# Later gather: selection columns written after all passes are planned, and zero fills moved from GpSimd to VectorE, in a decoder step with top-2-of-8 experts

## The chip, the cores and the metric

One core of a Trainium2 chip runs the whole program. The metric is device time in microseconds (us) of one execution, the median of several. The engines are TensorE (PE), VectorE (DVE), ScalarE (ACT), GpSimd (POOL) and the SyncE queue (SP) that issues most of the loads.

## What is computed

One inference step of two layers for 272 prompt rows (16 meta tokens and 256 tokens) and 8 sample rows, 280 rows of width 1024 in all. Layer 0 is a state-space and sparse-attention mixer with a dense SwiGLU. Layer 1 is a pooling mixer and then the part that matters here, a top-2-of-8 expert SwiGLU:

```
logits = (t @ router_w)                       # t: the normed rows, (280, 1024)
top_v, top_i = lax.top_k(logits, 2)
gates = jax.nn.softmax(top_v, axis=-1)
dense_gate = sum(one_hot(top_i, 8) * gates[..., None], axis=1)
for e in range(8):                            # expert width 3584
    out = out + dense_gate[:, e:e + 1] * (silu(t @ w_gate[e]) * (t @ w_up[e])) @ w_down[e]
```

## The kernel before

Rows are kept in three chunks (TC = 3) of 128, 128 and 24. The expert part works in passes. A pass takes up to 128 rows that chose one expert, so there are at least 8 passes, and up to 4 more where an expert has over 128 rows; the number is computed on the chip (`n_pass`). In a pass TensorE gathers the rows by a matmul with a 0/1 selection matrix `pick`, runs them through 84 blocks of weights, each split into a high and a low fp32r part (ScalarE copies the high part, L1502; VectorE subtracts it to get the low part, L2046; three matmuls each use them, L1153, L1157, L1158), and scatters the result back in the next pass through `pickTr`. The gather for pass i+1 is done inside pass i. The gather for pass 0 is done ahead of the loop, and it is this stretch that the change touches.

Each engine has its own instruction stream, written out by hand, with semaphores between them. `link(...)` on VectorE makes each small instruction wait for the one before. `filled(eng, x)` waits until TensorE has filled the PSUM bank of x, and `emptied(eng, x)` until that bank has been read. The streams before the loop, in their own order:

- VectorE: top-2 of the router logits (L1963 to L1974), then the low parts of the normed rows `hn4` (L1982); wait for `rank`, a running count of the rows of each expert (a matmul of TensorE, L1098); the place of each row within its expert, `slot_v` (L1986 to L1988); the selection columns `pick` for pass 0 from `slot_v` (L1990, three instructions), which signals `pick_ready`; the softmax gates (L1993 to L1998), which need the exponential of ScalarE (L1475, signal `router_exp`); the plan of the passes, in `pslot`, `pgate` and `exp_i` (L2002 to L2024), which signals `passes_ready`; the low parts of the gathered rows (L2029), which need ScalarE's high parts; a register load of the number of passes (L2039); the loop.
- TensorE: router logits (L1079); transposes of the normed rows into `h2n` (L1089); `rank` (L1098); transposes of the residual rows into `xn` (L1089 again); wait for `pick_ready`; gather half 0 and half 1, 20 matmuls each (L1108); wait for `late_zeros`; two matmuls on zeros that fill the `y` banks (L1133); wait for `passes_ready` and load the number of passes (L1134, L1135); the loop.
- ScalarE: high parts of `hn4` (L1473); the exponential (L1475); six copies of `xn` into the accumulator (L1480, by the helper at L1251); wait for gather half 0, high part; wait for gather half 1, high part (L1484); wait for `passes_ready`, load the number of passes (L1488, L1489); the loop, which begins with five high parts of weight blocks (L1502).
- GpSimd: waits until the last two `xn` banks are read, sets `pickTr` (128x384) and `ybr` (128x2048) to zero (L726, L727) and signals `late_zeros`.
- SP: the first 7 loads of expert weights (1 MB each) are issued before this stretch, so the loop's first blocks lie ready; the rest is issued as blocks are used.

Of the kernel before, what the change touches and what calls it, by code (L numbers as in the profile page):

```python
# [16 lines left out]
F32 = mybir.dt.float32  # L17
# [3 lines left out]
ALU = mybir.AluOpType  # L21
# [9 lines left out]
TC = 3  # L31
# [11 lines left out]
NE = 8  # L43
# [198 lines left out]
LOW_ROWS = 32  # L242
PASSES_EXTRA = 4
PASSES = NE + PASSES_EXTRA
# [36 lines left out]
def hybrid_step(nc, a, o):  # L281

    with ExitStack() as ctx:
        sems = {}

        def sem(name):
            if name not in sems:
                sems[name] = ctx.enter_context(nc.semaphore(name))
            return sems[name]
# [17 lines left out]
        pickTr = sb("pickTr", TC * P, F32R)  # L307
# [4 lines left out]
        ybr = sb("ybr", 2 * D, F32R)  # L312
# [8 lines left out]
        def const(name):  # L321
            at, n = CONST_AT[name]
            return consts[:, at:at + n]
# [18 lines left out]
        ident, ones, iota = const("ident"), const("ones"), const("iota")  # L342
# [107 lines left out]
        pick = pickr[:, :].rearrange("p (t s) -> p t s", t=TC)  # L450
# [13 lines left out]
        pslot = tk((PASSES + 1) * TC).rearrange("p (i t) -> p i t", i=PASSES + 1)  # L464
# [17 lines left out]
        def filled(eng, name):  # L482

            eng.wait_ge(bank_full[bank_of(name)], bank_uses(name))

        def emptied(eng, name):

            eng.wait_ge(bank_free[bank_of(name)], bank_uses(name))
# [29 lines left out]
        def ps(name):  # L518
            return bank[bank_of(name)]
# [156 lines left out]
        @block.gpsimd  # L676
        def _(pool):
            done = [0]

            def link(ins):  # L680

                done[0] += 1
                ins.then_inc(sem("pool_step"), 1)
                pool.wait_ge(sem("pool_step"), done[0])

            TT = nc.gpsimd.tensor_tensor
            nc.gpsimd.memset(eps, EPS)
            nc.gpsimd.memset(qibd, 0.0).then_inc(sem("zeroed"), 1)
            pool.wait_ge(sem("consts_in"), 16)
            nc.gpsimd.tensor_copy(hexp[0:H, :].rearrange("p (h m) -> p h m", h=H), ident[0:H, 0:H].unsqueeze(2).to_broadcast([H, H, HD]))  # L690
            nc.gpsimd.tensor_copy(hrep[0:H, :].rearrange("p (b h) -> p b h", b=NB),
                                  ident[0:H, 0:H].unsqueeze(1).to_broadcast([H, NB, H])).then_inc(sem("spread"), 1)

            pool.dma_start(o["pool_s"][:, 0:14, :], a["state_pool"][:, 1:15, :]).then_inc(sem("pool_old_out"), 16)

            for j in range(NJ):
                emptied(pool, ("bui", j))
                emptied(pool, ("bur", j))
                gr, gi = g4[:, j % 2, 0, :], g4[:, j % 2, 1, :]
                TT(pt[0], er3[:, j, :], gr, ALU.mult)  # L700
                TT(pt[1], ei3[:, j, :], gi, ALU.mult)
                TT(pt[2], er3[:, j, :], gi, ALU.mult)
                link(TT(pt[3], ei3[:, j, :], gr, ALU.mult))
                TT(er3[:, j, :], pt[0], pt[1], ALU.subtract)
                TT(ei3[:, j, :], pt[2], pt[3], ALU.add).then_inc(sem("states"), 1)
                pool.wait_ge(sem("states"), j + 1)

            emptied(pool, "kidT")
            for t in range(TC):
                pool.dma_start(o["kidx"][t * P:t * P + TCN[t], :], z3["kid"][0:TCN[t], t, :]).then_inc(sem("ki_out"), 16)  # L710
            for t in range(TC):
                for n, name in (("v", ("v", t)), ("k", ("kt", t))):
                    emptied(pool, name)
                    pool.dma_start(o[n][t * P:t * P + TCN[t], :], z3[n][0:TCN[t], t, :]).then_inc(sem("kv_out"), 16)
            filled(pool, ("y", 3))
            nc.gpsimd.memset(psbd, 0.0).then_inc(sem("probs_zeroed"), 1)
            pool.wait_ge(sem("sample_state"), 1)
            pool.dma_start(o["hs"], hs.rearrange("p j r b -> p (j r b)")).then_inc(sem("state_out"), 16)
            pool.wait_ge(sem("last_state"), 1)
            pool.dma_start(o["hl"], hlast).then_inc(sem("state_out"), 16)  # L720
            pool.wait_ge(sem("mixer_over"), 1)
            emptied(pool, "svT")
            pool.dma_start(hist.rearrange("p c b r -> p (c b r)"), a["hist"]).then_inc(sem("hist_in"), 16)
            for i in range(2):
                emptied(pool, ("xn", 2, i))
            nc.gpsimd.memset(pickTr[:, :].bitcast(F32), 0.0)  # L726
            nc.gpsimd.memset(ybr[:, :].bitcast(F32), 0.0).then_inc(sem("late_zeros"), 1)  # L727

        @block.tensor
        def _(pe):  # L730
# [819 lines left out]
        def _(dve):  # L1550
# [3 lines left out]
            def link(ins):  # L1554

                done[0] += 1
                ins.then_inc(sem("dve_step"), 1)
                dve.wait_ge(sem("dve_step"), done[0])
# [418 lines left out]
            for t in range(TC):  # L1977
                for i in range(2):
# [2 lines left out]
                    low_rows = hn4[0:n, 1, t, cols] if t < 2 else hn4[LOW_ROWS:LOW_ROWS + n, 0, t, cols]  # L1981
                    TT(low_rows, ps(("h2n", t, i))[0:n, :], hn4[0:n, 0, t, cols].bitcast(F32),  # L1982
                       ALU.subtract).then_inc(free(("h2n", t, i)), 1)
            filled(dve, "rank")
            rp = ps("rank")[:, 0:4 * NE].rearrange("p (t e) -> p t e", t=4)
            link(TT(slot_v, sel, rp[:, 0:TC, :], ALU.mult))  # L1986
            link(TS(slot_v, slot_v, -1.0, None, ALU.add))
            link(nc.vector.tensor_copy(slot_v[LOW_ROWS:LOW_ROWS + 24, 2, :], slot_v[0:24, 2, :]))  # L1988
            for t in range(TC):
                last = TS(pick[:, t, :], iota, slot_v[:, t, 0:1], None, ALU.is_equal)  # L1990
            last.then_inc(sem("pick_ready"), 1)
            dve.wait_ge(sem("router_exp"), 1)
            link(TS(g12[:, 2, :], g12[:, 1, :], 1.0, None, ALU.add))  # L1993
            link(nc.vector.reciprocal(g12[:, 2, :], g12[:, 2, :]))
# [1 line left out]
            link(TT(oh1, oh1, g12[:, 2, :].unsqueeze(2).to_broadcast([P, TC, NE]), ALU.mult))  # L1996
            link(TT(oh2, oh2, g12[:, 3, :].unsqueeze(2).to_broadcast([P, TC, NE]), ALU.mult))
            link(TT(gate, oh1, oh2, ALU.add))  # L1998

            ov2 = over.rearrange("p (b e) -> p b e", b=2)  # L2000
            for b in range(2):
# [11 lines left out]
            for dst, src, first in ((pslot[:, 0:PASSES, :], cand, slot_v), (pgate[:, 1:PASSES + 1, :], gcand, gate)):  # L2013
# [3 lines left out]
                link(nc.vector.tensor_reduce(dst[:, NE:PASSES, :].rearrange("p i t -> p t i"), prod, AX.X, ALU.add))  # L2017
                link(nc.vector.tensor_copy(dst[:, 0:NE, :].rearrange("p e t -> p t e"), first))
            link(TT(prod[:, 0, :, :], const("ecol").unsqueeze(1).to_broadcast([P, 4, 16]), oh, ALU.mult))
            link(nc.vector.tensor_copy(pexp[:, 0:NE], iota[:, 0:NE]))  # L2020
            link(nc.vector.tensor_reduce(pexp[:, NE:PASSES], prod[:, 0, :, :], AX.X, ALU.add))
            link(nc.vector.tensor_copy(exp_i[:, 0:PASSES], pexp))
            link(TS(over[:, 0:1], ranko[:, 15:16], float(NE), None, ALU.add))
            nc.vector.tensor_copy(exp_i[:, PASSES:PASSES + 1], over[:, 0:1]).then_inc(sem("passes_ready"), 1)  # L2024
            dve.wait_ge(sem("passes_ready"), 1)
            for half in range(2):
                cs = slice(4 * half, 4 * half + 4)
                dve.wait_ge(sem("high_copied"), half + 1)
                TT(xg4[:, 1, cs, :], bank[PASS_BANK[("gather", half)]][:, :].rearrange("p (c s) -> p c s", c=4),  # L2029
                   xg4[:, 0, cs, :].bitcast(F32), ALU.subtract).then_inc(bank_free[PASS_BANK[("gather", half)]], 1)  # L2030
# [162 lines left out]
```

## Time and profile before

| | us |
|---|---|
| median of 3 runs | 1674.99 |
| lowest, highest | 1674.94, 1676.63 |
| profiled execution, its time | 1674.94 |
| profiled execution, its span | 1673.1 |
| TensorE busy | 1566.4 (94%) |
| VectorE busy | 1272.2 (76%) |
| ScalarE busy | 963.8 (58%) |
| GpSimd busy | 89.3 (5%) |

The profile is of one execution. Its times count from the start of the span; 1.8 us of the execution's own time lie outside the span. "L1990" is a line of the kernel before. PEclk is the granted clock of TensorE, where 1.00 is 2.4 GHz and 0.50 is 1.2 GHz.

### The profile page before, as it was taken

Reading aid. Unit: us, or ns where it says so; the run is one execution under the profiler, and the core shown is the slowest. Engines: PE = TensorE matmul, PEld = TensorE weight load, DVE = VectorE, ACT = ScalarE, POOL = GpSimd, SP = SyncE. Lnnn points to the kernel's source line nnn. Section 1 sums busy time; section 2 is a strip of 40 time slices with the busy share of each in tenths; the row PEclk is TensorE's granted clock in tenths of the full one; section 3 lists DMA queues with packets and bytes.
Section 4 is the critical chain, followed back from the end, with each engine's and each line's share of the span. In section 5 each row is a group of like instructions: output and inputs, shape, how many; then the busy total and the mean of one; then the engine's idle time right before and its main releaser. Section 6 shows DMA issues by size and latency. Waiting matters only on the chain.

```text
span 1673.1 us, 23394 instructions
## 1 busy us (share of the span) xinstructions
PE 1566.4 (94%) x7789; PEld 1263.8 (76%) x7789; DVE 1272.2 (76%) x1702; ACT 963.8 (58%) x1222; POOL 89.3 (5%) x120
## 2 busy tenths in 40 slices
PE   5997858889999878999999999999999999999998
PEld 4653436479999767888888888888888888888887
DVE  8888561135554469988988988988998998988986
ACT  2110314124443227777777777777777777777774
POOL 0386100000000000000000000000000000000000
PEclk9998778999999979999999999999999999999999
DMA  5421012524545516998998998998998998998992
GB/s 219 151 76 51 30 54 64 150 101 152 193 128 173 180 59 241 361 363 311 358 373 301 355 369 307 355 374 309 346 366 320 351 366 319 348 363 323 350 357 92
DMA packets 212886, 420.79 MB, mean 252 GB/s; under 512 B 10233, under 2 KB 56469, under 8 KB 212572
## 3 DMA queue, kind: packets, MB, share of 16 engines
q1 hardware_dynamic: 211542, 414.37, 68.9%
q10 hardware_dynamic: 622, 3.45, 0.5%
q0 software_dynamic: 672, 2.32, 0.4%
q8 instruction: 30, 0.49, 0.1%
q14 instruction: 20, 0.16, 0.0%
HBM read 417.50 MB, written 3.07 MB: 251 GB/s over the span
## 4 chain that ended last, share of the span: by engine, by line
PE 83%; DVE 4%; issue 2%; ACT 1%; DMA 1%; SPq 1%; ACTq 0%; DVEq 0%
PE bank L1153 19%; PE bank L1158 19%; PE bank L1157 19%; PE bank L1034 3%; PE bank L1031 3%; PE bank L1035 3%; PE bank L1108 2%; PE bank L1014 2%; PE bank L1178 1%; PE bank L1116 1%; PE bank L1046 1%; PE bank L1050 1%; PE bank L1049 1%; PE bank L748 1%; PE bank L922 1%
## 5 line engine op out<-in xcount | busy, mean ns | idle before, releaser
L2046 DVE TENSOR_TENSOR split<-raw_w,split 128x1024 fp32r<-128x1024 f32 x672 | 783.3, 1220 | 50.3 <-ACT split L1502 48.2
L1502 ACT ACTIVATE split<-raw_w 128x1024 fp32r<-128x1024 f32 x672 | 684.2, 1059 | 109.1 <-PE bank L1153 108.1
L1153 PE MATMUL bank<-split,xgr 128*128 128x512 f32 x896 | 359.2, 401 | 6.0 <-DVE split L2046 6.0
L1158 PE MATMUL bank<-split,xgr 128*128 128x512 f32 x896 | 354.3, 395 | 0.0
L1157 PE MATMUL bank<-split,xgr 128*128 128x512 f32 x896 | 354.2, 395 | 0.0
L1153 PEld LDWEIGHTS bank<-split,xgr 128*128 128x128 f32 x896 | 169.3, 189 | 43.8 <-DVE split L2046 6.4
L1158 PEld LDWEIGHTS bank<-split,xgr 128*128 128x128 f32 x896 | 169.0, 189 | 39.9
L1157 PEld LDWEIGHTS bank<-split,xgr 128*128 128x128 f32 x896 | 169.4, 189 | 37.5
L1153 PE MATMUL bank<-split,hbr 128*128 128x512 f32 x448 | 177.9, 397 | 0.0
L1158 PE MATMUL bank<-split,hbr 128*128 128x512 f32 x448 | 176.9, 395 | 0.0
L1157 PE MATMUL bank<-split,hbr 128*128 128x512 f32 x448 | 176.9, 395 | 0.0
L1031 PE MATMUL bank<-split 128*128 128x280 f32 x352 | 103.6, 294 | 6.5 <-DVE split L1902 6.5
L1035 PE MATMUL bank<-split 128*128 128x280 f32 x352 | 103.4, 294 | 0.0
L1034 PE MATMUL bank<-split 128*128 128x280 f32 x352 | 103.3, 294 | 0.0
L1428 ACT ACTIVATE split<-ring 128x1024 fp32r<-128x1024 f32 x44 | 46.4, 1059 | 92.3 <-PE bank L1031 70.5
L1158 PEld LDWEIGHTS bank<-split,hbr 128*128 128x128 f32 x448 | 84.3, 188 | 20.0
L1153 PEld LDWEIGHTS bank<-split,hbr 128*128 128x128 f32 x448 | 84.3, 188 | 19.3
L1157 PEld LDWEIGHTS bank<-split,hbr 128*128 128x128 f32 x448 | 84.3, 188 | 19.2
L1892 DVE TENSOR_TENSOR split<-ring,split 128x1024 fp32r<-128x1024 f32 x44 | 53.8, 1226 | 51.1 <-ACT split L1428 51.1
L2052 DVE TENSOR_TENSOR hbr<-bank,hbr 128x512 fp32r<-128x512 f32 x56 | 38.6, 690 | 49.3 <-ACT hbr L1507 49.3
L1532 ACT ACTIVATE late<-bank 128x512 f32<-128x512 f32 x56 | 33.5, 598 | 71.4 <-PE bank L1158 71.4
L1031 PEld LDWEIGHTS bank<-split 128*128 128x128 f32 x352 | 67.2, 191 | 6.9 <-issue 6.9
(377 smaller groups left out, 1904.2 us busy)
## 6 DMA issues: line engine op xcount, KB each, us to landing
raw_w<-in_moe_gate SPq DMA_DIRECT2D x112, 1024.0 KB, 5.4
raw_w<-in_moe_up SPq DMA_DIRECT2D x112, 1024.0 KB, 6.1
raw_w<-in_moe_down SPq DMA_DIRECT2D x112, 1024.0 KB, 5.1
ring<-in_w_gate SPq DMA_DIRECT2D x11, 1024.0 KB, 5.0
ring<-in_w_up SPq DMA_DIRECT2D x11, 1024.0 KB, 7.3
ring<-in_w_down SPq DMA_DIRECT2D x8, 1408.0 KB, 6.2
ring<-in_w_in SPq DMA_DIRECT2D x5, 2048.0 KB, 9.6
ring<-in_w_out SPq DMA_DIRECT2D x2, 2048.0 KB, 7.8
```

The source lines that it names most:

```text
L1031: first = mm(out[:, 0:T], w[0][:, c, :], xs[:, 0, c, :], start=(c == 0), stop=False)
L1034: mm(out[:, 0:T], w[0][:, c, :], xs[:, 1, c, :], start=False, stop=False)
L1035: last = mm(out[:, 0:T], w[1][:, c, :], xs[:, 0, c, :], start=False, stop=(c == C - 1))
L1153: first = mm(out, hi, place[:, s, 0, cols], start=start, stop=False)
L1157: mm(out, lo, place[:, s, 0, cols], start=False, stop=False)
L1158: last = mm(out, hi, place[:, s, 1, cols], start=False, stop=stop)
L1428: A(place[:, n % FF_PLACES, 0, :].rearrange("p (c m) -> p c m", c=C), unit(name, 256)[:, k * C:(k + 1) * C, (f % 2) * P:(f % 2) * P + P], ...
L1502: A(place[:, s, 0, :], raw_w[:, at:at + BLOCK], ACT.Copy).then_inc(sem("high_ready"), 1)
L1532: A(th[:, j % 2, :], bank[b][:, :], ACT.Silu).then_inc(bank_free[b], 1)
L1892: TT(low_, unit(f"ffn{f // 2}", 256)[:, k * C:(k + 1) * C, (f % 2) * P:(f % 2) * P + P], high.bitcast(F32), ALU.subtract).then_inc(sem("ff ...
L2046: TT(place[:, s, 1, :], raw_w[:, at:at + BLOCK], place[:, s, 0, :].bitcast(F32), ALU.subtract).then_inc(sem("low_ready"), 1)
L2052: TT(dst, src, high.bitcast(F32), ALU.subtract).then_inc(bank_free[PASS_BANK[name]], 1)
```

## The change

On VectorE the gate arithmetic now comes before the wait for `rank`. `slot_v` is computed after it. The plan of the passes follows as before, with one copy of 24 rows made on `pslot` in place of the one made on `slot_v`. Only after `passes_ready` are the selection columns of pass 0 written, now read from `pslot`, and `pick_ready` signalled. Then VectorE, in place of GpSimd, waits for the two `xn` banks and sets `pickTr` and `ybr` to zero. The low parts of the gathered rows follow. The streams of TensorE, ScalarE and SP are as before.

```
@@ gpsimd
             pool.dma_start(hist.rearrange("p c b r -> p (c b r)"), a["hist"]).then_inc(sem("hist_in"), 16)
-            for i in range(2):
-                emptied(pool, ("xn", 2, i))
-            nc.gpsimd.memset(pickTr[:, :].bitcast(F32), 0.0)
-            nc.gpsimd.memset(ybr[:, :].bitcast(F32), 0.0).then_inc(sem("late_zeros"), 1)
@@ vector
-            filled(dve, "rank")
-            rp = ps("rank")[:, 0:4 * NE].rearrange("p (t e) -> p t e", t=4)
-            link(TT(slot_v, sel, rp[:, 0:TC, :], ALU.mult))
-            link(TS(slot_v, slot_v, -1.0, None, ALU.add))
-            link(nc.vector.tensor_copy(slot_v[LOW_ROWS:LOW_ROWS + 24, 2, :], slot_v[0:24, 2, :]))
-            for t in range(TC):
-                last = TS(pick[:, t, :], iota, slot_v[:, t, 0:1], None, ALU.is_equal)
-            last.then_inc(sem("pick_ready"), 1)
             dve.wait_ge(sem("router_exp"), 1)
             link(TS(g12[:, 2, :], g12[:, 1, :], 1.0, None, ALU.add))
...
             link(TT(gate, oh1, oh2, ALU.add))
+
+            filled(dve, "rank")
+            rp = ps("rank")[:, 0:4 * NE].rearrange("p (t e) -> p t e", t=4)
+            link(TT(slot_v, sel, rp[:, 0:TC, :], ALU.mult))
+            link(TS(slot_v, slot_v, -1.0, None, ALU.add))
...
             link(TT(prod[:, 0, :, :], const("ecol").unsqueeze(1).to_broadcast([P, 4, 16]), oh, ALU.mult))
+            link(nc.vector.tensor_copy(pslot[LOW_ROWS:LOW_ROWS + 24, 0:PASSES, 2], pslot[0:24, 0:PASSES, 2]))
             link(nc.vector.tensor_copy(pexp[:, 0:NE], iota[:, 0:NE]))
...
             nc.vector.tensor_copy(exp_i[:, PASSES:PASSES + 1], over[:, 0:1]).then_inc(sem("passes_ready"), 1)
             dve.wait_ge(sem("passes_ready"), 1)
+            for t in range(TC):
+                last = TS(pick[:, t, :], iota, pslot[:, 0, t:t + 1], None, ALU.is_equal)
+            last.then_inc(sem("pick_ready"), 1)
+            for i in range(2):
+                emptied(dve, ("xn", 2, i))
+            nc.vector.memset(pickTr[:, :].bitcast(F32), 0.0)
+            nc.vector.memset(ybr[:, :].bitcast(F32), 0.0).then_inc(sem("late_zeros"), 1)
             for half in range(2):
                 cs = slice(4 * half, 4 * half + 4)
                 dve.wait_ge(sem("high_copied"), half + 1)
```

## Rows read from the trace of the kernel before

**Rows 1.** The page's busy time of each engine, with share and instructions

```profile
PE 1566.4 (94%) x7789; PEld 1263.8 (76%) x7789; DVE 1272.2 (76%) x1702; ACT 963.8 (58%) x1222; POOL 89.3 (5%) x120
```

**Rows 2.** Busy time by stretch, one pass; columns as in the first line

```profile
core 0: us, PE busy (x) PEld busy (x) DVE busy (x) ACT busy (x) POOL busy (x), PEclk, DMA share, GB/s
752.00:880.00 128.00, 128.00 (x589) 104.65 (x588) 113.20 (x114) 97.57 (x106) 0.00 (x0) 1.00 0.94 345
```

**Rows 3.** Chain that ended last, 625 to 644 us: start, length, engine, tile, line

```profile
625.11 0.19 DVE late L1986
...
625.54 0.17 DVE late L1988
...
625.73 0.68 DVE pickr L1990 x3
626.41 0.09 DVE late L1993
...
633.82 0.17 DVE small_i L2024
...
634.00 0.47 ACTq L1489
...
636.29 1.07 ACT split L1502
...
637.38 1.24 DVE split L2046
...
638.66 0.79 PE bank L1153
639.45 0.43 PE bank L1157
...
643.73 0.23 PE bank L1153
```

**Rows 4.** Timeline of ScalarE, 622 to 635 us; [idle before, released by]

```profile
622.72 1.07 ACT L1473 ACTIVATE hnr<-bank 24x512 fp32r<-24x512 f32 x2 [0.26 <-PE bank L1089]
623.80 1.28 ACT L1475 ACT_TABLE_LOAD   x1
625.10 0.20 ACT L1475 ACTIVATE late<-late 128x3 f32<-128x3 f32 x1
...
632.20 0.60 ACT L1484 ACTIVATE xgr<-bank 128x512 fp32r<-128x512 f32 x1 [1.63 <-PE bank L1108]
635.00 1.28 ACT L1502 ACT_TABLE_LOAD   x1 [2.20 <-issue]
```

**Rows 5.** Timeline of TensorE, 618 to 633 us

```profile
618.15 5.01 PE L1089 MATMUL bank<-consts,hT 128*128 128x128 f32 x24
...
624.93 2.82 PE L1089 MATMUL bank<-consts,xT 128*128 128x128 f32 x24
627.50 4.66 PE L1108 MATMUL bank<-pickr,hnr 128*128 128x128 f32 x40
632.00 0.68 PE L1133 MATMUL bank<-ybr 128*128 128x512 f32 x2
```

**Rows 6.** Busy time by stretch, columns as in rows 2, where PEclk changes

```profile
604.00:605.00 1.00, 0.47 (x2) 0.03 (x1) 0.00 (x0) 0.49 (x1) 0.00 (x0) 1.00 0.92 332
...
609.00:610.00 1.00, 0.00 (x0) 0.00 (x0) 1.00 (x4) 0.00 (x0) 0.00 (x0) 0.50 0.00 0
...
622.00:623.00 1.00, 1.00 (x8) 0.72 (x6) 0.91 (x2) 0.74 (x2) 0.00 (x0) 0.68 0.00 0
...
636.00:636.50 0.50, 0.00 (x0) 0.00 (x0) 0.00 (x0) 0.49 (x2) 0.00 (x0) 0.80 0.00 0
...
643.00:643.50 0.50, 0.50 (x3) 0.36 (x2) 0.50 (x2) 0.50 (x2) 0.00 (x0) 0.87 1.08 422
```

**Rows 7.** Timeline of VectorE, a large zero fill and the gathered low parts

```profile
610.92 1.76 DVE L1954 MEMSET hnr<- 128x2048 f32 x1 [0.49 <-DVE hT L1565]
...
634.00 1.29 DVE L2029 TENSOR_TENSOR xgr<-bank,xgr 128x512 fp32r<-128x512 f32 x2
```

**Rows 8.** VectorE's sequencer at L2039: count, ns, first and last start

```profile
L2039 DVEq TENSOR_LOAD <-small_i x1: 552/552/552, 634.0 to 634.0; - x1
```

## The prediction, made before the changed kernel ran

> **What bounds the kernel now.** I read the page first: TensorE is busy 94% of the span, VectorE 76% [rows 1]. An average hides stages, so I then took the busy time by stretch over each pass of the expert loop. Seven stretches of a pass each, from 752 to 1648 us, read alike; one of them stands in the rows: TensorE is busy 128.00 of 128 us at full clock [rows 2]. The loop is bound by TensorE and has no gap that could absorb a late start. DMA is at 0.94 of its share there, close to a bound, but it never leaves TensorE idle. So whatever moves the first expert matmul, at 638.66 us, moves the end by the same amount.
>
> Then I read the chain of waits that ends in that first matmul [rows 3]. It runs on VectorE alone from 625.11 (first use of `rank`) to the end of L2024 at 633.97, which signals `passes_ready`. From there: ScalarE loads the number of passes (634.00), loads an activation table from 635.00 to 636.28 [rows 4], makes the first high part (636.29, 1.07), VectorE makes its low part (637.38, 1.24), and TensorE starts at 638.66. From signal to matmul that is 638.66 - 633.97 = 4.69 us.
>
> The gather of pass 0 is not on that chain. `pick` is ready at 626.41 [rows 3], the gather runs from 627.50 to 632.16 [rows 5], and ScalarE's second copy ends at 632.80 [rows 4], 1.2 us before `passes_ready`. The planning of the passes hides the gather. That cover is what the change takes away.
>
> **The change part by part.**
>
> *The planning chain, up to `passes_ready`.* Removed between `rank` and `passes_ready`: the copy of 24 rows and the three selection instructions, from 625.54 to the start of the gate arithmetic. L1993 began inside the last selection: the chain shows 0.09 us of it after 626.41, and an instruction of its size takes about 0.17 (L1988), so it began near 626.33. That is 0.79 us [rows 3]. Added: a copy of 24 rows on `pslot`, which I price like the old one with its hand-over, 0.2 [rows 3]; and a wait, since the gates now come first and need the exponential, which ends at 625.10 + 0.20 = 625.30 [rows 4] where `rank` let the chain start at 625.11 [rows 3], so 0.2. Behind that waiting instruction on VectorE stands all the planning, so all of it shifts. The order of gates and `slot_v` among themselves costs nothing, as every instruction is linked to the one before either way. Net: -0.79 + 0.2 + 0.2 = -0.4, and `passes_ready` comes at 633.6.
>
> *The selection columns.* Now behind `passes_ready`, three instructions, 0.68 us as before [rows 3]. They read another tile of the same kind. `pick_ready`: 633.6 + 0.02 + 0.68 = 634.3. TensorE wakes about 0.04 later (the step from L2046 to L1153 in the chain [rows 3]), so the gather starts at 634.35 in place of 627.50.
>
> *The gather.* 40 matmuls. At full clock they took 4.66 us, 0.1165 each [rows 5]. But TensorE has now been idle since the `xn` transposes ended at 627.75 [rows 5], 6.6 us. The granted clock went to 0.50 by 609.0 after a last matmul at 604.47, so within 4.5 us, and at 636.30 after TensorE ended at 632.68, so after 3.6 us [rows 5, 6]. 6.6 us is more than both, so the gather starts at 1.2 GHz. The clock came back at 622.64 (a mean of 0.68 over that us is 0.64 us at 0.50 and 0.36 at 1.00; the other times are read in the same way) and at 643.13 [rows 6], about 4.5 us after dense work began at 618.15 [rows 5] and at 638.66 [rows 3]. No gather at low clock stands in the trace. The nearest rows are the 24 transposes of the same width, 128 columns: at full clock 2.82 us, 0.1175 each, which is what a gather matmul costs there; and 5.01 us for the 24 that began at 618.15 [rows 5]. Of these, those after 622.64, some 0.5 us and 4 matmuls, ran at full clock, so 20 or 21 took 4.5 us, 0.218 each. I take 0.218 for the gather. In 4.5 us that makes 20.6 matmuls; the other 19.4 at 0.1165 take 2.3. Sum 6.8 us, and the gather ends at 634.35 + 6.8 = 641.15. The bounds: 4.7 if the clock is high throughout, 8.7 if it is low throughout.
>
> *From the gather to the loop.* ScalarE's stream has the two gather copies ahead of its wait for `passes_ready`, so it is stuck there until the second half is in its bank. Behind it are the register load, the table load and every high part of the loop; behind those are VectorE's low parts and TensorE. The second copy starts at 641.2. Does the register load wait for this 0.60 us copy? VectorE's sequencer did its own load at 634.0 [rows 8] while L2029 was computing from 634.00 to 635.29 [rows 7], so a sequencer runs ahead of its engine, and I take it that the copy hides the register load's start. From 641.2 the same 4.69 us as before follow (register load, table, high part, low part): first expert matmul at 645.9. If the sequencer does not run ahead, add 0.6.
>
> For that table load the Trainium skill ("ScalarE: Activation LUTs", What ACT_TABLE_LOAD costs) states a drain of about 1.38 us besides the load's 1.28. The trace does not agree: the load at 623.80 begins as the copies of `hn4` end at 623.79, and the exponential follows it at 625.10 [rows 4]. By the page's figure the load would come an estimated 0.9 us later here, because ScalarE is now busy just before it.
>
> *Zero fills.* Off GpSimd's and onto VectorE: 128x2048 took VectorE 1.76 us [rows 7], so with 128x384 in proportion 2.1 us, from 634.3 to 636.5. The banks they wait for are read long before. Behind them on VectorE stand the low parts of the gathered rows, but these need ScalarE's copies at 641 to 642; hidden by the gather. Without that cover they would cost the 2.1. The low parts then end near 642.5, and TensorE wants them at 645.9; hidden by ScalarE's table load. The two matmuls on zeros (L1133) follow the gather within 0.7 us [rows 5]; hidden too, as is TensorE's own register load.
>
> *The loop's start.* Before, about ten matmuls ran at 0.43 in place of 0.23 until the clock rose [rows 3], 2 us lost. After the change TensorE idles from about 641.7 to 645.9, 4.2 us, which is longer than one of the two idle times after which the clock fell (3.6) and shorter than the other's bound (4.5) [rows 5, 6]. I take the fall as likelier, with the same 2 us lost: no difference.
>
> **Sum.** 645.9 - 638.66 = +7.2 us. Made up from the pieces: gather end moves from 632.16 to 641.15 (+9.0), and of this the 1.8 us by which the old gather ended ahead of `passes_ready` are eaten up first. On the profiled execution's 1674.94 that is 1682.1; the median shown is 1674.99, so it is the same for it.
>
> **Rivals.**
>
> *The clock stays up (not as far as I say).* The 4.2 us of idling before the loop do not bring the clock down, so the ten slow matmuls at the start run at 0.23. For it: the gather now sits right before the loop, and one fall came only by 4.5 us. Against it: the other came after 3.6. Price -2.0: 1680.1. A part of it, an earlier rise in the loop or in the gather, lies between.
>
> *A longer way from gather to loop.* The register load waits for the copy (+0.6), or the gather stays at low clock throughout (+1.9). For it: there is no row of a gather at low clock. Against it: the sequencer row, and both rises came 4.5 us after dense work began. 1682.7 to 1684.0.
>
> *The late gather is hidden anyway (not slower).* If something else held the loop back until after the gather, only the shorter planning chain would count: -0.4, 1674.6. This decides if the gather's second half is in its bank by 633.6, or if the loop could give the time back. For it: DMA is at 0.94 in the loop, so a ring of weights that has had more time to fill is the only thing that gains. Against it: the ring is already full at the start, TensorE has no idle time in any pass [rows 2], and the gather would have to end before `pick` exists.
>
> **How the numbers follow.** About 0.2% (3.3 us) is what a measurement of this kernel can tell from no change. Chances: my sum, 1681.2 to 1682.6, 0.6; clock up, near 1680, 0.2; longer way 0.12; hidden 0.05, within 0.2%; something that I don't see 0.03. The range that leaves out less than 2 in 10 is 1679.7 to 1684.1: its low end is the clock's rival less a little for an early rise in the gather, its high end the gather at low clock throughout. Slower by over 0.2% means above 1678.3, which takes in the first three cases: 0.93. Same 0.05, faster 0.02.
>
> **What would show it.** In the changed profile: `passes_ready` 0.3 to 0.5 us earlier; L1108's first 40 matmuls starting near 634.4 with a PEclk of 0.50 for the first 4 to 5 us; ScalarE's second gather copy near 641.2; its table load near 642 and not before; the first L1153 near 645.9; passes of unchanged length after that; the zero fills on VectorE ended before the gather is. The prediction would be wrong if the gather started at full clock, if ScalarE loaded the number of passes ahead of its gather copies, or if a pass of the loop became shorter or longer.

## The result and the profile after

The changed kernel is slower: 1689.7 us median of four timed runs (1686.3 to 1692.9) against 1675.8 for the kernel before (one run more than in the table above), a ratio of 1.0081 with a 95% interval of 1.0054 to 1.0108. Timed again in six runs beside the kernel before in 23, it took 1688.3 against 1677.4, ratio 1.0063 (1.0041 to 1.0085). The forecast was 1682.1 with a range of 1679.7 to 1684.1. The direction was right, the size was not. The profiled execution took 1684.85 us, 9.91 more than that of before.

Line numbers differ a little from those of the kernel before: the gather is now L1104, the first expert matmul L1149, ScalarE's gather copies L1480, the loop's high parts L1498.

The page's busy times of the changed kernel, to be set beside [rows 1]: TensorE runs the same 7789 matmuls, so the added time is waiting and low clock.

```profile
PE 1571.4 (93%) x7789; PEld 1268.0 (75%) x7789; DVE 1274.4 (76%) x1704; ACT 963.7 (57%) x1222; POOL 87.2 (5%) x118
```

The chain that ended last, changed kernel, 625 to 645 us (start, length, engine, tile, line):

```profile
625.39 0.21 ACT late L1471
...
625.62 0.18 DVE late L1981
...
626.89 0.19 DVE late L1990
...
633.74 0.17 DVE small_i L2018
...
633.93 0.04 DVE pickr L2021
...
634.62 0.27 issue
634.90 8.78 PE bank L1104 x40
643.68 0.02 issue
643.70 0.48 ACT xgr L1480
```

In [rows 3] this chain was VectorE's planning alone and the gather was not on it. Now it starts with the exponential (L1471), runs through the gates (L1981) and the planning to L2018, and then through the gather, which alone is 8.78 us.

TensorE over the same stretch, changed kernel:

```profile
610.99 7.73 PE L1075 MATMUL bank<-params,hT 128*128 128x8 f32 x48 [6.01 <-DVE hT L1561]
618.66 4.75 PE L1085 MATMUL bank<-consts,hT 128*128 128x128 f32 x24
623.25 2.07 PE L1094 MATMUL bank<-late,consts 128*128 128x8 f32 x18
625.18 2.82 PE L1085 MATMUL bank<-consts,xT 128*128 128x128 f32 x24
634.90 8.77 PE L1104 MATMUL bank<-pickr,hnr 128*128 128x128 f32 x40 [6.90 <-DVE pickr L2021]
643.46 1.16 PE L1129 MATMUL bank<-ybr 128*128 128x512 f32 x2
648.37 0.80 PE L1149 MATMUL bank<-split,xgr 128*128 128x512 f32 x1 [3.75 <-DVE split L2047]
```

Against [rows 5], the 40 matmuls of the gather take 8.77 us in place of 4.66, after 6.90 us in which TensorE waited for the selection columns. The first expert matmul is at 648.37 in place of 638.66.

Busy time by stretch, changed kernel (columns as in [rows 2]): where the clock fell, the gather, where the clock rose, and one pass of the loop.

```profile
632.00:633.00 1.00, 0.00 (x0) 0.00 (x0) 0.86 (x5) 0.00 (x0) 0.00 (x0) 0.93 0.00 0
...
634.90:643.67 8.77, 8.77 (x41) 8.77 (x42) 2.58 (x3) 0.60 (x1) 0.00 (x0) 0.50 0.00 0
...
653.00:654.00 1.00, 1.00 (x6) 0.77 (x5) 1.00 (x3) 1.00 (x2) 0.00 (x0) 0.83 1.05 410
...
763.00:891.00 128.00, 128.00 (x590) 104.65 (x589) 113.20 (x114) 97.48 (x105) 0.00 (x0) 1.00 0.94 344
```

The granted clock is 0.50 over the whole gather, and over everything from 632.86 (a mean of 0.93 over that us) to 653.34. In [rows 6] the fall at 636.30 was followed by a rise at 643.13. The passes of the loop are as in [rows 2].

ScalarE and VectorE after the gather, changed kernel:

```profile
643.70 0.60 ACT L1480 ACTIVATE xgr<-bank 128x512 fp32r<-128x512 f32 x1 [3.67 <-PE bank L1104]
644.71 1.28 ACT L1498 ACT_TABLE_LOAD   x1 [0.41 <-issue]
646.00 4.84 ACT L1498 ACTIVATE split<-raw_w 128x1024 fp32r<-128x1024 f32 x5
```

```profile
634.64 0.38 DVE L2025 MEMSET pickTr<- 128x384 f32 x1
635.39 1.76 DVE L2026 MEMSET ybr<- 128x2048 f32 x1 [0.38 <-issue]
640.06 0.69 DVE L2030 TENSOR_TENSOR xgr<-bank,xgr 128x512 fp32r<-128x512 f32 x1 [2.90 <-ACT xgr L1480]
644.33 0.69 DVE L2030 TENSOR_TENSOR xgr<-bank,xgr 128x512 fp32r<-128x512 f32 x1 [3.57 <-ACT xgr L1480]
```

The table load begins 1.01 us after the second gather copy began and 0.41 after it ended; from the copy's start to the first expert matmul it is 648.37 - 643.70 = 4.67 us. The zero fills are over at 637.15, long before the low parts can start.

**How profiles are compared here.** Executions differ before this stretch is reached: the router's first matmul (the one after the 6.01 us of idling) came between 610.1 and 618.2 us of the span in the profiles below, also in kernels whose code up to there is that of before. So two distances are used: from the router's first matmul to the first expert matmul, and from it to the end of the span.

| kernel | router's first matmul | to first expert matmul | to end of span |
|---|---|---|---|
| before | 610.48 | 28.18 | 1062.6 |
| changed | 610.99 | 37.38 | 1072.0 |
| changed, profiled again | 614.09 | 37.65 | 1072.5 |

By this the change costs 9.4 us, or 9.9 by its second profile. The two profiles of one kernel differ by 0.3 and 0.5 us, so a single difference of that size between two kernels says little. Of the 9.91 between the two profiled executions, 0.51 arose before the router.

### The profile page after: what moved, and what is told of

It reads as the page before. It is cut to its first block, busy times and chain, and to the rows that moved or that the text cites. A ratio compares the mean times of both kernels' runs of the same rounds, so it can differ in the third digit from the quotient of the medians.

```text
span 1683.0 us, 23394 instructions
## 1 busy us (share of the span) xinstructions
PE 1571.4 (93%) x7789; PEld 1268.0 (75%) x7789; DVE 1274.4 (76%) x1704; ACT 963.7 (57%) x1222; POOL 87.2 (5%) x118
## 4 chain that ended last, share of the span: by engine, by line
PE 83%; DVE 3%; issue 2%; ACT 1%; DMA 1%; SPq 0%; DVEq 0%; ACTq 0%
PE bank L1149 19%; PE bank L1154 19%; PE bank L1153 19%; PE bank L1027 3%; PE bank L1030 3%; PE bank L1031 3%; PE bank L1104 3%; PE bank L1010 2%; PE bank L1174 1%; PE bank L1112 1%; PE bank L1042 1%; PE bank L1046 1%; PE bank L1045 1%; PE bank L744 1%; DVE hT L1561 1%
## 5 line engine op out<-in xcount | busy, mean ns | idle before, releaser
L1498 ACT ACTIVATE split<-raw_w 128x1024 fp32r<-128x1024 f32 x672 | 684.4, 1060 | 109.3 <-PE bank L1149 108.1
L1149 PE MATMUL bank<-split,xgr 128*128 128x512 f32 x896 | 359.2, 401 | 3.7 <-DVE split L2047 3.7
L1149 PEld LDWEIGHTS bank<-split,xgr 128*128 128x128 f32 x896 | 169.3, 189 | 41.9 <-DVE split L2047 4.5
L1149 PE MATMUL bank<-split,hbr 128*128 128x512 f32 x448 | 177.9, 397 | 0.0
L1149 PEld LDWEIGHTS bank<-split,hbr 128*128 128x128 f32 x448 | 84.3, 188 | 19.3
```

The source lines that it names most:

```text
L1149: first = mm(out, hi, place[:, s, 0, cols], start=start, stop=False)
L1498: A(place[:, s, 0, :], raw_w[:, at:at + BLOCK], ACT.Copy).then_inc(sem("high_ready"), 1)
```

## The experiments

Eleven runs follow. Where nothing else is said, the diff is against the changed kernel.

### The changed kernel again

No edit.

> The changed kernel once more, unaltered. The profiled execution of it took 1684.85 us with the clock low in one stretch from 632.9 to 653.3 us of the span, and four timed ones 1686.3, 1687.1, 1692.3 and 1692.9. Theory A (the extra time is the late gather and its clock alone): every execution has the same low stretch of about 20 us, and the times gather within 2 us of 1685. Theory B (the low stretch differs from execution to execution, by whether the clock has come back when the expert loop is under way): the times spread over 5 us and more, and a slower one shows a mean granted clock some 0.002 to 0.004 lower, that is 7 to 14 us more at 1.2 GHz.

Measured: 1688.3 us median, 1684.5 to 1692.6. TensorE in its profile:

```profile
614.09 7.74 PE L1075 MATMUL bank<-params,hT 128*128 128x8 f32 x48 [6.02 <-DVE hT L1561]
...
638.27 8.76 PE L1104 MATMUL bank<-pickr,hnr 128*128 128x128 f32 x40 [6.83 <-DVE pickr L2021]
...
651.74 0.80 PE L1149 MATMUL bank<-split,xgr 128*128 128x512 f32 x1 [3.75 <-DVE split L2047]
```

The gather repeats to 0.01 us, with the clock low throughout, and the low stretch was again 20.5 us (636.7 to 657.1). The first expert matmul is 37.65 us after the router's first. The times spread over 8 us all the same, but so do those of the kernel before timed beside them, 1674.1 to 1682.8. This profiled execution took 1688.44; 3.1 of the 3.6 us above the first one had arisen before the router. Neither theory held as I put it. As theory B has it, the times spread over more than 5 us and the slower executions show the lower mean clock (0.952 at 1692.6 us, 0.957 at 1684.5). But the low stretch around the gather is equally long in both profiles, and most of the difference between them lies ahead of it.

### Only the late selection, fills back on GpSimd

```
@@ gpsimd
+            for i in range(2):
+                emptied(pool, ("xn", 2, i))
+            nc.gpsimd.memset(pickTr[:, :].bitcast(F32), 0.0)
+            nc.gpsimd.memset(ybr[:, :].bitcast(F32), 0.0).then_inc(sem("late_zeros"), 1)
@@ vector
-            for i in range(2):
-                emptied(dve, ("xn", 2, i))
-            nc.vector.memset(pickTr[:, :].bitcast(F32), 0.0)
-            nc.vector.memset(ybr[:, :].bitcast(F32), 0.0).then_inc(sem("late_zeros"), 1)
```

> The changed kernel with its two zero fills back on GpSimd, where they were before; the selection columns of pass 0 stay behind the planning. Theory A (the late gather is the cost): nothing of the loss comes back, first expert matmul at 648.3 us within 0.5, time as the changed kernel's within 1 us. Rival (the fills on VectorE, 2.1 us, ahead of the low parts of the gathered rows are a good part of the cost): 2 us or more faster than the changed kernel.

Measured: 1685.5 us median of six, ratio to before 1.0048 (1.0032 to 1.0064). The median is 2.7 us under that of the changed kernel run again (1688.3), which the expectation had named as the rival's sign. But those six times lie from 1684.5 to 1692.6, and the distances, 37.29 and 1072.0, are those of the changed kernel within 0.1 of its first profile and 0.5 of its second. By the distances the late selection alone carries the whole loss; the position named in the expectation, 648.3, was 647.4, since the router stood 0.9 us earlier.

### Only the fills on VectorE (against the kernel before)

```
@@ gpsimd
-            for i in range(2):
-                emptied(pool, ("xn", 2, i))
-            nc.gpsimd.memset(pickTr[:, :].bitcast(F32), 0.0)
-            nc.gpsimd.memset(ybr[:, :].bitcast(F32), 0.0).then_inc(sem("late_zeros"), 1)
@@ vector
             dve.wait_ge(sem("passes_ready"), 1)
+            for i in range(2):
+                emptied(dve, ("xn", 2, i))
+            nc.vector.memset(pickTr[:, :].bitcast(F32), 0.0)
+            nc.vector.memset(ybr[:, :].bitcast(F32), 0.0).then_inc(sem("late_zeros"), 1)
```

> The kernel before with only the two zero fills moved to VectorE, behind the signal that the passes are planned; the selection columns are written early as before. Theory A: gather at 627.5 to 632.2 us as before, first expert matmul at 638.7 within 0.4 (the low parts of the gathered rows end near 637.5 in place of 635.3, about when the first high part of the loop is ready), time within 0.5 us of the kernel before. Rival (fills on the path): first expert matmul 2 us later, 1677.

Measured: ratio 0.9999 (0.9984 to 1.0013). Distances 28.54 and 1062.9: +0.36 at the first expert matmul, within the 0.4 expected. Its profiled execution took 1682.91 us, and the profile shows that 7.7 us of this lay ahead of the router (618.16 against 610.48).

TensorE's clock in this profile bears on what follows. The same gather ran here at full clock, with 4.53 us of idling behind it in place of the two matmuls on zeros:

```profile
632.66 2.82 PE L1085 MATMUL bank<-consts,xT 128*128 128x128 f32 x24
635.24 4.66 PE L1104 MATMUL bank<-pickr,hnr 128*128 128x128 f32 x40
644.43 1.22 PE L1129 MATMUL bank<-ybr 128*128 128x512 f32 x2 [4.53 <-DVE ybr L2025]
```

The granted clock fell at 640.7 (a mean of 0.85 over the us from 640), only 0.8 us after the gather had ended and 5.2 us after the last transpose. In the five profiles in which TensorE idled after the same transposes (the changed kernel twice, the late selection alone, dense columns, transposes) it fell 4.8 to 5.2 us after the last of them. So in this one profile the clock fell as early as if the gather had not run.

### The changed kernel with a warm gather

```
+            b = PASS_BANK[("gather", 0)]
+            pe.wait_ge(bank_free[b], BEFORE_FILL[b])
+            for _ in range(30):
+                mm(bank[b][:, :], hn4[:, 0, 0, 0:P], hn4[:, 0, 0, 0:512], start=True, stop=True)
             pe.wait_ge(sem("pick_ready"), 1)
```

> The changed kernel with 30 matmuls of 512 columns put into TensorE's idle time between the transposes of the residual rows and the wait for the selection columns; their result is overwritten. At 0.23 us each they take 7 us. If the low clock is what made the gather 8.6 us long, it now takes 4.7 us from near 634.9, the first expert matmul comes 4 us earlier than in the changed kernel, near 644.4, and its time falls by 4 us or more, and if the runs of 1692 us come from the gather as well, the spread goes too. Rival (the gather is long because of its operands or of memory traffic, not of the clock): the gather still takes 8.6 us at a granted clock of 1.00.

Measured: ratio to before 1.0032 (1.0018 to 1.0046), 1682.7 us median. TensorE, and its clock during the gather:

```profile
612.86 7.73 PE L1075 MATMUL bank<-params,hT 128*128 128x8 f32 x48 [6.01 <-DVE hT L1565]
...
629.62 7.07 PE L1123 MATMUL bank<-hnr 128*128 128x512 f32 x30
636.55 4.68 PE L1104 MATMUL bank<-pickr,hnr 128*128 128x128 f32 x40
...
645.93 0.80 PE L1153 MATMUL bank<-split,xgr 128*128 128x512 f32 x1 [4.18 <-DVE split L2051]
```

```profile
636.55:641.23 4.68, 4.68 (x42) 4.68 (x42) 2.81 (x3) 0.60 (x1) 0.00 (x0) 1.00 0.01 4
```

The same gather in the same place takes 4.68 us at full clock, so the low clock is what made them 8.77. Distances 33.07 and 1068.0: 4.3 and 4.0 us come back, where the expectation said 4. The spread did not go (1679.3 to 1688.1), which fits the reading that it has another source.

### Only the gates moved ahead (against the kernel before)

```
+            dve.wait_ge(sem("router_exp"), 1)
+            link(TS(g12[:, 2, :], g12[:, 1, :], 1.0, None, ALU.add))
...
+            link(TT(gate, oh1, oh2, ALU.add))
             filled(dve, "rank")
...
             last.then_inc(sem("pick_ready"), 1)
-            dve.wait_ge(sem("router_exp"), 1)
-            link(TS(g12[:, 2, :], g12[:, 1, :], 1.0, None, ALU.add))
...
-            link(TT(gate, oh1, oh2, ALU.add))
```

> The kernel before with one part of the change alone: the gate arithmetic stands ahead of the wait for the running count, and the selection columns are still written early, right after the places of the rows. Theory A (the order of the planning costs nothing, the late gather everything): the gather starts by 628.5 us (counted with the router's first matmul at 610.5), is over before the planning is, and the time is that of the kernel before within 0.3 us (+0.2 for the wait on the exponential). Rival (the reordering itself delays the planning by 1 us or more): first expert matmul 1 us or more later.

Measured: ratio 0.9996 (0.998 to 1.0012). The gather starts 17.77 us after the router's first matmul, which is 628.25 counted from 610.48; distances 28.50 and 1062.9. By the distances the reordering costs 0.3 us, no more than two profiles of one kernel differ by; the timing, with an interval of 0.16% either way, can't tell it from nothing.

### Dense columns in the late gather

```
-                gather_half(half, bank[b])
+                gather_half(half, bank[b], hn4[:, 0, 0, 0:P])
```

`gather_half` takes this third argument as the moving operand in place of `pick[:, t, :]`.

> The changed kernel with the moving operand of the first gather replaced: the same 40 matmuls of 128 columns read rows of data where the 0/1 selection columns stood, so the first pass gathers sums of no meaning. In two profiled executions of the changed kernel the gather began at 1.2 GHz and ended at 1.2 GHz after 8.6 us, though the clock had come back within 4.5 us of the start of the transposes. Theory C (what the selection columns hold, mostly zeros, is why the clock does not come back): here it comes back within the gather, and the gather takes 6 to 7.5 us. Theory D (it is the form and spacing of these matmuls): 8.6 us at 1.2 GHz again.

Measured: ratio 1.0049 (1.0027 to 1.0072); distances 37.60 and 1072.5. The gather and its clock:

```profile
640.43 8.77 PE L1104 MATMUL bank<-hnr 128*128 128x128 f32 x40 [6.83 <-DVE pickr L2022]
```

```profile
640.43:649.19 8.76, 8.76 (x41) 8.76 (x42) 2.61 (x3) 0.60 (x1) 0.00 (x0) 0.50 0.00 0
```

Theory C falls: what the columns hold made no difference.

### Transposes in place of the late gather

```
-                gather_half(half, bank[b])
+                for k in range(20):
+                    last = nc.tensor.transpose(bank[b][:, (k // 5) * P:(k // 5 + 1) * P],
+                                               hn4[:, 0, 0, 0:P].bitcast(F32), ident)
+                last.then_inc(bank_full[b], 1)
```

> The changed kernel with the 40 matmuls of its first gather replaced by 40 transposes of one 128x128 block of the normed rows, so the first pass gathers no rows. My sum took its rate and its clock from transposes of that width; neither selection columns nor dense columns brought the clock back in a gather. Theory D (the kind of matmul decides): the transposes start at 1.2 GHz after the same idle time, the clock comes back 3.5 to 6 us after their start, and they end within 6 to 7.5 us. Rival (after this idle time nothing brings it back in 8 us): 1.2 GHz to the end, 8.5 us.

One execution, 1687.8 us. The 40 transposes, and two stretches in them:

```profile
640.38 6.91 PE L1125 MATMUL bank<-consts,hnr 128*128 128x128 f32 x40 [6.88 <-DVE pickr L2024]
```

```profile
644.00:645.00 1.00, 1.00 (x7) 1.00 (x6) 0.00 (x0) 0.08 (x1) 0.00 (x0) 0.50 0.00 0
645.00:646.00 1.00, 1.00 (x10) 1.00 (x9) 0.45 (x1) 0.52 (x1) 0.00 (x0) 0.89 0.00 0
```

The clock was low from 638.4, came back at 645.2, 4.8 us after the transposes began, and they took 6.9 us. Theory D held. 6.9 us is what my sum gave for the gather, 6.8. First expert matmul 35.51 us after the router's first, 7.3 more than before; the sum had 7.2. Here the clock, up since 645.2, fell again at 652.0, 4.3 us after the last of the two matmuls on zeros. These transposes differ from the gather in more than one way: they are fp32 where the gather is fp32r, they are issued as transposes, and they use one block throughout where the gather takes a new one each time. The last is hardly it, since the 24 transposes behind the router take a new block each and brought the clock back in every profile. Between the other two nothing decides.

### TensorE kept at work before the loop (against the kernel before)

```
                 mm(bank[b][:, :], yb3[:, 0, 0:P], yb3[:, 0, 0:512], start=True, stop=True).then_inc(bank_full[b], 1)
+            b = PASS_BANK[("gate", 0)]
+            pe.wait_ge(bank_free[b], BEFORE_FILL[b])
+            for _ in range(24):
+                mm(bank[b][:, :], hn4[:, 0, 0, 0:P], hn4[:, 0, 0, 0:512], start=True, stop=True)
```

> The kernel before with 24 matmuls of 512 columns, their result overwritten, put between the two on zeros and the loop, about 5.6 us of work in TensorE's idle time from 632.7 to 638.7. If the low clock at the loop's start (4.5 us in the profile of before) costs what the rows say, it goes, the first expert matmul stays at 638.7 (28.2 us after the router's first), and the end comes 2.0 us earlier, a ratio of 0.9988, which the timing hardly tells from 1; the profile's PEclk of 1.00 from 623 us to the end shows it. Rival (the added matmuls themselves delay the loop): first expert matmul later than 28.5 us after the router's first.

Measured: ratio 0.9984 (0.9968 to 0.9999). No low clock between 626.2 and 1674 us. Distances 28.34 and 1061.6, so 1.0 us comes back at the end where I expected 2.0. The scatter matmuls of the loop (L1116) show where the rest went. Counted from the first expert matmul, the first scatter comes at 5.67 us against 7.71 before, 2.04 earlier, which is the price that I had put on the low clock. The second comes at 12.43 against 14.21, the third at 25.62 against 26.73, 1.11 earlier, and there the difference stays. So 0.9 us is given back within the first 26 us of the loop. The two other kernels with this gap filled have the same third scatter, at 25.62. VectorE is busy 19.88 of the first 20 us there, so its low parts are a likely limit, but that was not tried.

### Both gaps filled in the changed kernel

The 30 matmuls of the warm gather and 17 like those above.

> The changed kernel with TensorE kept at work in both gaps: 30 matmuls of 512 columns before the late gather and 17 between the two on zeros and the loop. If the loss is made up of the gather and its wait in the path (which stays) and of two stretches at low clock (which go), then: first expert matmul 33.1 us after the router's first, as with the first gap filled alone, no low clock after 625 us, and from the router's first matmul to the end of the span some 1.5 to 2.5 us less than with the first gap filled alone (1068.1), so 1065.6 to 1066.6, against 1062.65 before. Rival (the added matmuls delay the loop): first expert matmul later than 33.5.

Measured: ratio 1.0026 (1.0009 to 1.0042). Distances 33.37 and 1066.7, both just above what was expected, and no low clock after 628 us. So without any low clock the late selection still costs 4.1 us against the kernel before, and 5.0 against the kernel before with its own gap filled.

### The opposite of the change (against the kernel before)

```
             last.then_inc(sem("pick_ready"), 1)
-            dve.wait_ge(sem("router_exp"), 1)
...
-            link(TT(gate, oh1, oh2, ALU.add))
             ov2 = over.rearrange("p (b e) -> p b e", b=2)
...
                 link(STT(oh[:, k, :], ranko, float(k + 1), over, ALU.is_equal, ALU.mult))
+            link(TT(prod[:, 0, :, :], const("ecol").unsqueeze(1).to_broadcast([P, 4, 16]), oh, ALU.mult))
...
+            nc.vector.tensor_copy(exp_i[:, PASSES:PASSES + 1], over[:, 0:1]).then_inc(sem("passes_ready"), 1)
+            dve.wait_ge(sem("router_exp"), 1)
...
+            link(TT(gate, oh1, oh2, ALU.add))
             for b in range(2):
                 link(TS(cand[:, :, b, :], slot_v, -128.0 * (b + 1), None, ALU.add))
...
-            link(TT(prod[:, 0, :, :], const("ecol").unsqueeze(1).to_broadcast([P, 4, 16]), oh, ALU.mult))
...
-            nc.vector.tensor_copy(exp_i[:, PASSES:PASSES + 1], over[:, 0:1]).then_inc(sem("passes_ready"), 1)
```

> The opposite of the change: in the kernel before, only what the number of passes and their experts need is computed between the selection columns and the signal that the passes are planned; gates, slots and the rest of the plan follow the signal. Theory A (what sets the loop's start is whichever is later, the gather with its copies or the planning signal, and then 4.7 us): the signal comes near 629.5, the gather copies end at 632.8 as before and the table load follows at once, first high part at 634.1; VectorE is done with its own work near 635.3, so the first expert matmul is near 636.6 in place of 638.7, 2.0 us earlier, and the time falls by 1.5 to 2.5 us. Rival (the 4.7 us are bound to something else, such as the register loads): no gain.

Measured: ratio 0.9988 (0.9971 to 1.0004); distances 26.13 and 1061.2. ScalarE:

```profile
634.09 0.60 ACT L1484 ACTIVATE xgr<-bank 128x512 fp32r<-128x512 f32 x1 [1.38 <-PE bank L1108]
636.32 0.60 ACT L1484 ACTIVATE xgr<-bank 128x512 fp32r<-128x512 f32 x1 [1.64 <-PE bank L1108]
637.32 1.28 ACT L1502 ACT_TABLE_LOAD   x1 [0.40 <-issue]
```

The planning signal now comes at 633.2, ahead of the second gather copy, and the gather has become the later of the two even at full clock. The first expert matmul, at 640.99, is again 4.67 us after the start of that copy. It comes 2.05 us earlier than before, as expected; of that, 1.4 is left at the end. The interval of the timing still takes in 1. The expectation had the signal near 629.5 counted as in the profile of before; it came at 628.8 by that count, also ahead of the gather's end.

### The opposite, with the gap filled

The edit above and 14 matmuls in the gap.

> The kernel before with the number of passes computed first (2.05 us earlier at the first expert matmul) and 14 matmuls of 512 columns in the gap before the loop. It joins two changes that each gave something: router's first matmul to end of span 1061.23 with the first alone, 1061.63 with 24 matmuls in the gap alone. If they add, 1059.5 to 1060.3, and the time 2.5 to 3.5 us under the kernel before, ratio 0.998. Rival (at full clock the first blocks of the loop wait for VectorE's low parts, so the clock gives nothing on top): 1061.2.

Measured: 1675.9 us median against 1677.7, ratio 0.9981 (0.9967 to 0.9995). TensorE:

```profile
613.52 7.74 PE L1079 MATMUL bank<-params,hT 128*128 128x8 f32 x48 [6.01 <-DVE hT L1569]
...
630.58 4.66 PE L1108 MATMUL bank<-pickr,hnr 128*128 128x128 f32 x40
635.08 0.67 PE L1133 MATMUL bank<-ybr 128*128 128x512 f32 x2
635.59 3.38 PE L1137 MATMUL bank<-hnr 128*128 128x512 f32 x14
639.95 0.51 PE L1157 MATMUL bank<-split,xgr 128*128 128x512 f32 x1 [0.98 <-DVE split L2050]
```

Distances 26.43 and 1059.7: 2.9 us under the kernel before and 12.3 under the changed one. The two parts add within 0.5 us. The timed medians show 1.8 us under the kernel before, less than the 2.5 to 3.5 expected, with an interval of 0.8 to 5.5. This version beats both.

## Why the prediction was wrong in size

**The bound and the lost cover: right.** The loop is bound by TensorE and passes a late start on: from first expert matmul to end of span 1034.4 us before, 1034.6 after. The late selection alone gives the whole loss, 37.29 against 37.38, and the fills and the reordering alone give some 0.3 us each, about what two profiles of one kernel differ by.

**The planning chain and the selection: right.** Forecast `passes_ready` 0.4 us earlier: counted from the router it is 0.6 earlier (23.49 to 22.90). The handover to TensorE took 0.3 us, not the 0.04 that I took from a matmul in the loop's chain. The two cancel: gather start 23.9 us after the router's first matmul, forecast and measured.

**The gather: the step that failed.** The sum had the low clock for the first 20.6 of the 40 matmuls: "In 4.5 us that makes 20.6 matmuls; the other 19.4 at 0.1165 take 2.3. Sum 6.8 us". The rate was right, 0.214 each at low clock (634.90 to 643.46) against the 0.218 that I took. The return of the clock was not. I took it from the transposes and from the loop's 512-column matmuls. The transposes cost the same per instruction at full clock, but they are no measure for the clock's return: transposes in the gather's place bring the clock back 4.8 us in and end after 6.9; the gather, with 0/1 columns or dense ones, stayed at 1.2 GHz to its end in all four profiles that entered it at low clock. The bound "8.7 if it is low throughout" was the case that came, 8.6 to 8.8, and I had given this case, with another, 0.12. It is +2.0 us on the forecast +7.2.

**From the gather to the loop: right.** 4.67 us from the start of the second copy to the first expert matmul, within 0.01 in all nine profiles in which the gather was the later of the two, against 4.69. ScalarE's register load did start with the copy. The drain of 1.38 us that the Trainium skill states ("ScalarE: Activation LUTs", What ACT_TABLE_LOAD costs) is not seen: the load begins 0.41 us after the copy ends and the first high part follows the load at once.

**The loop's start: nearly.** The clock was low there, as forecast, but for 5.0 us in place of 4.5, +0.2 at the end (the second profile has 5.4). The 2 us that I put on such a low stretch hold at the first scatter, but only 1.1 of them come back at the end when the gap is filled, so the rival "the clock stays up" was priced too high. That I had it falling again was beside the point in the changed kernel, since it never rose; in the run with transposes it did rise and did fall.

**The sum.** 7.2 forecast; +2.0 for the gather (8.80 from its start to the second copy in place of 6.85) and +0.2 for the longer low stretch at the loop's start: 9.4, as measured on distances in the first profile.

**The rivals.** A gather at low clock throughout, one half of "a longer way from gather to loop", is what came; its other half, a register load that waits for the copy, did not. The clock did not stay up before the loop, as it had never come up, and nothing hid the gather.

**The range.** The mis-sized gather puts the time at 1674.94 + 9.4 = 1684.3, just past the range's upper end of 1684.1. The median of 1689.7 lies 5 us beyond, and these fit the spread of the program rather than the change: the kernel before, shifted by 9.4, would lie from 1683.5 to 1692.6, and the changed kernel's eleven executions lie from 1684.5 to 1692.9. I took three runs within 1.7 us for the spread of this program. Over all its runs the kernel before took from 1674.1 to 1683.2 us, and the profiles put the difference ahead of the router: router at 610.48 in an execution of 1674.94 us, 613.75 in one of 1677.23, 615.62 in one of 1680.28, 618.16 in one of 1682.91, all of kernels with nearly the same distance from there. The execution of before on which I built was one of the fastest. Busy time by stretch of two of them, kernel before and then fills on VectorE, shows where it begins: a lower granted clock in the first stretch and between 250 and 370 us. From 370 to 490 us it is lower too, 0.97 against 1.00, while from 120 to 250 us it is higher, 0.78 against 0.75.

```profile
0.00:120.00 120.00, 96.47 (x380) 67.54 (x381) 102.85 (x233) 21.78 (x67) 46.09 (x63) 0.97 0.43 155
...
250.00:370.00 120.00, 104.46 (x510) 69.91 (x509) 24.21 (x59) 35.51 (x90) 0.55 (x1) 0.90 0.36 110
```

```profile
0.00:120.00 120.00, 98.38 (x374) 69.39 (x375) 99.47 (x226) 21.53 (x65) 43.24 (x59) 0.94 0.42 150
...
250.00:370.00 120.00, 108.22 (x506) 72.19 (x502) 22.09 (x73) 36.40 (x104) 0.55 (x1) 0.87 0.35 110
```

The same link shows over whole executions: of the 78 timed ones of the kernel before beside the experiments, those under 1675.5 us have a mean granted clock of 0.960 or 0.961, and those above 1682 have 0.955 to 0.957. Why the clock differs between executions of the same code was not tried. That it is the clock which makes all of the 7.7 us is argued from these means, not shown.

## What to carry to other kernels

A small matmul block that hides behind another engine's chain costs about its own length when it is moved behind that chain, and more if the clock falls in the wait. Here 4.7 us of gather cost 4.1 to 5.0 us with both gaps filled and 9.4 without: TensorE's clock fell while it waited, the gather ran at 0.214 us a matmul in place of 0.117, and everything behind ScalarE's copies of the gather came after it. When a low clock is priced, ask what kind of work brought it back in the row at hand, and price the case that it does not come back. And what can be computed for another engine's sake should be computed first: sending the number of passes ahead of the rest of the plan, and keeping TensorE at work in the gap, took 2.9 us off the kernel before by the distances, where the change put 9.4 on.

## What was not expected of the hardware

Forty fp32r matmuls of 128 columns, each with its own weights, ran for 8.8 us at 1.2 GHz without the clock coming back, in all four profiles that entered them at low clock, with 0/1 and with dense data alike. Forty transposes of the same width had it back after 4.8 us (one profile), and the 24 transposes behind the router did in all thirteen profiles, 3.9 to 4.8 us after their start. The 512-column matmuls at the start of the loop took 3.5 to 6.0 us (the run with transposes; the opposite of the change). The router's 48 matmuls of 8 columns, 7.7 us of work, ran at low clock throughout in every profile. And once, behind a gather at full clock, the clock fell 0.8 us after the gather's end (fills on VectorE). Whether fp32 against fp32r decides or the transposing was not separated.
